# A hybrid decoder layer on one core: the attention half of the out-projection summed ahead of the delta rule, with weight buffers reused by halves

## What is computed

```python
def hybrid_mixer(...):
    proj = x @ w_in                                   # q_a k_a v_a | q_d k_d v_d | b a z
    o_attn = sliding_window_sink_attention(q_a, k_a, v_a, attn_sinks)      # 512 columns
    o_dn = gated_delta_rule(q_d, k_d, v_d, g, beta)                        # 512 columns
    o_dn = rms_norm(o_dn) * dn_norm_g * silu(z_d)
    return jnp.concatenate([o_attn, o_dn], axis=-1) @ w_out                # 1024 x 1024
...
h = layer_norm(alpha * h + mix, ln1_g, ln1_b)
ffn = peer_ffn(h, peer_w_query, sub_keys, expert_u, expert_v)
h = layer_norm(alpha * h + ffn, ln2_g, ln2_b)
```

## Time and profile before

| what | us |
|---|---|
| median of 3 runs | 3261.68 |
| the profiled execution, its own time | 3272.0 |
| its span, first to last instruction | 3270.2 |
| PE busy (matmul) | 2437.8 (75%) |
| DVE busy | 2231.2 (68%) |
| POOL busy | 1183.3 (36%) |
| ACT busy | 1140.2 (35%) |
| mean granted TensorE clock | 0.872 of full speed |

### The profile page before, as it was taken

How to read it: one execution, slowest core, us unless ns; L and a number is a source line. 1 busy time by engine, 2 the same in 40 slices (tenths; PEclk the granted TensorE clock), 3 DMA queues, 4 the chain that set the end, 5 groups by cost and what they waited for, 6 DMA issues and landing times.

```text
span 3270.2 us, 37892 instructions
## 1 busy us (share of the span) xinstructions
PE 2437.8 (75%) x11896; PEld 1362.5 (42%) x11896; DVE 2231.2 (68%) x5593; ACT 1140.2 (35%) x3499; POOL 1183.3 (36%) x1028
## 2 busy tenths in 40 slices
PE   8888778867788677877778777776778667776554
PEld 7675335534356233543446433553345323341111
DVE  3367765896559865797558875588656986579444
ACT  3213532344332533335233353234423253322222
POOL 0022543244422444334432344333443244333452
PEclk9899898988999888888989898997899879887777
DMA  8069999999999999999999999999999999989997
GB/s 331 13 235 399 408 421 397 384 394 383 398 403 396 384 415 404 385 403 379 421 383 398 388 402 398 387 379 396 386 407 383 392 387 415 397 350 356 421 421 315
DMA packets 189000, 1235.90 MB, mean 378 GB/s; under 512 B 21752, under 2 KB 21880, under 8 KB 54656
## 3 DMA queue, kind: packets, MB, share of 16 engines
q0 software_dynamic: 147456, 1073.81, 80.9%
q1 hardware_dynamic: 39168, 154.32, 12.0%
q10 hardware_dynamic: 2176, 5.36, 0.4%
HBM read 1229.21 MB, written 4.19 MB: 377 GB/s over the span
## 4 chain that ended last, share of the span: by engine, by line
PE 35%; DMA 26%; DVE 20%; ACT 9%; issue 8%; POOL 2%; DVEq 0%; POOLq 0%; ACTq 0%; SPq 0%
DMA ring<-in_uv,expert_used 22%; PE expert_sum L880 15%; DVE ring L1557 9%; PE bank L587 8%; PE bank L576 5%; DMA chunk<-in_weights 4%; POOL ring L526 2%; ACT diag L1138 2%; PE bank L594 1%; PE bank L704 1%; DVE arena L1280 1%; ACT arena L997 1%; ACT h_raw L1131 1%; PE bank L599 1%; ACT L1131 1%
## 5 line engine op out<-in xcount | busy, mean ns | idle before, releaser
L526 POOL DMA_INDIRECT ring<-in_uv,expert_used x1024 | 1183.1, 1155 | 2056.1 <-PE expert_sum L880 1568.2
L880 PE MATMUL expert_sum<-ring,diag 128*64 128x512 f32 x4096 | 1208.1, 719 | 686.6 <-ACT diag L1138 686.1
L1557 DVE CUSTOM_DVE_ANT_0 ring<-ring,x_pair 128x1024 f32<-128x1024 f32 x1024 | 1230.6, 1223 | 567.7 <-DMA ring<-in_uv,expert_used 562.4
L880 PEld LDWEIGHTS expert_sum<-ring,diag 128*64 128x64 f32 x4096 | 313.2, 156 | 1329.7 <-issue 1315.8
L1131 ACT ACTIVATE h_raw<-h_raw 128x2 f32<-128x2 f32 x512 | 104.2, 204 | 1555.6 <-DVE h_raw L1557 1554.7
L1138 ACT ACTIVATE diag<-const,h_raw 128x64 f32<-128x64 f32 x1024 | 292.7, 333 | 1.8 <-PE expert_sum L880 1.8
L1134 ACT ACTIVATE h_raw<-h_raw,gate_used 128x1 f32<-128x1 f32 x1024 | 245.6, 286 | 16.7
L587 PEld LDWEIGHTS bank<-oT,chunk 128*128 128x128 f32 x1376 | 156.4, 192 | 22.7 <-issue 22.7
L587 PE MATMUL bank<-oT,chunk 128*128 128x128 f32 x1376 | 162.4, 277 | 0.0
L576 PE MATMUL bank<-chunk,oT 128*128 128x256 f32 x464 | 116.6, 401 | 31.4 <-DMA chunk<-in_weights 30.6
L1280 DVE MAX8 arena<-arena 128x8 f32<-128x128 f32 (+1 forms) x384 | 103.8, 326 | 41.4 <-ACT arena L1089 36.2
(11 more groups left out here) (255 smaller groups left out, 2663.3 us busy)
## 6 DMA issues: line engine op xcount, KB each, us to landing
chunk<-in_weights SPq DMA_DIRECT2D x228, 512.0 KB, 10.7
ring<-in_weights SPq DMA_DIRECT2D x16, 1024.0 KB, 18.8
ring<-in_uv,expert_used POOLq DMA_INDIRECT x1024, 11.5
chunk<-in_weights SPq DMA_DIRECT2D x5, 1024.0 KB, 19.6
x<-in_x SPq DMA_DIRECT2D x8, 512.0 KB, 13.7
out<-oT ACTq DMA_DIRECT2D x8, 512.0 KB, 8.4
o_cat<-in_xT SPq DMA_DIRECT2D x7, 512.0 KB, 15.2
xT_even<-in_xT SPq DMA_DIRECT2D x4, 512.0 KB, 10.0
```

The costliest lines, as they stand in the source:

```text
L526: pool.indirect_dma_start(out=ring[:, (j % RING) * 2 * D:(j % RING + 1) * 2 * D], out_offset=None, in_=io["uv"], in_offset=bass.IndirectOf ...
L880: mm = pe.matmul(expert_sum[i][c * SPAN:(c + 1) * SPAN, :], diag[:, (j % DIAGS) * SPAN:(j % DIAGS + 1) * SPAN], ring3[:, j % RING, D + i * ...
L1557: dve.tensor_tensor_reduce(u, u, x_pair[:, (j % 2) * D:(j % 2 + 1) * D], 1.0, 0.0, ALU.mult, ALU.add, h_raw[:, j:j + 1]).then_inc(dotted.s ...
```

## The change

1. PE turns attention's half of `o_cat` right after mark att_o (it waits for `att_out`, and uses bank 5); ACT copies it to `oT` after its copies of the keys and values, ahead of the work of norms.
2. Between the marks norms and decay, PE makes the sums over k-tiles 0 to 3 of all four out-chunks, into banks 4 and 5. This takes the place of `keep_busy(early, 6)` of block 0.
3. DVE adds alpha times x to them (two operations) right after L1379, ahead of mark decay; the kk matmuls into bank 5 wait for this (`half_added`).
4. After the delta rule PE turns only the second half of `o_cat` and sums over k-tiles 4 to 7 only. DVE's two operations there stay, as plain additions.
5. Weight halves become units of their own: four places of 512 KB, used in turn, each half loaded when the half four loads earlier has been used. The order for the out-projection is the first halves of its four chunks, then the second halves.
6. One pair each moves from marks norms and decay to softmax and turn_p.

```diff
 EARLIER = dict(
-    rope=1, gates=1, taps1=1, scores=2, taps2=1, softmax=1, turn_p=1, att_o=2,
-    norms=2, decay=2, kk=1, ...
+    rope=1, gates=1, taps1=1, scores=2, taps2=1, softmax=2, turn_p=2, att_o=2,
+    norms=1, decay=1, kk=1, ...
...
+        def half_place(g):
+
+            return chunk[g % 4 // 2][:, g % 2 * KT * W // 2:(g % 2 + 1) * KT * W // 2]
...
             def load(g):
-                c = LOADS[g][0]
-                before = LOADS[g - 2] if g > 1 else (...)
-                for half in range(2):
-                    cols = slice(half * KT * W // 2, (half + 1) * KT * W // 2)
-                    if half == 0:
-                        sp.wait_ge(half_used, USED[before])
-                    else:
-                        sp.wait_ge(*used(*before))
-                    alone(sp)
-                    sp.dma_start(chunk[g % 2][:, cols], io["weights"][c][:, cols]).then_inc(chunk_in[g % 2][half], 16)
+                c, _, half = LOADS[g]
+                if g > 3:
+                    last = LOADS[g - 4]
+                    sp.wait_ge(half_used, HALF_USED[last[0], last[1], last[2]])
...
+                alone(sp)
+                sp.dma_start(half_place(g), io["weights"][c][:, half * KT * W // 2:(half + 1) * KT * W // 2]).then_inc(half_in[g % 4], 16)
...
-                for c in range(IN_CHUNKS, CHUNKS):
+                for half in range(2):
+                    for c in range(IN_CHUNKS, IN_CHUNKS + OUT_CHUNKS):
+                        load(LOAD_OF[c, n + 1, half])
+                for c in range(IN_CHUNKS + OUT_CHUNKS, CHUNKS):
                     if c not in KEPT:
-                        load(LOAD_OF[c, n + 1])
+                        for half in range(2):
+                            load(LOAD_OF[c, n + 1, half])
...
+            def half_tokens_out(m, c, out, act, half):
+
+                half_there(c, m, half)
+                w, ks = half_of(c, m, half), HALVES[half]
+                for k in ks:
+                    mm = pe.matmul(out, act[:, k, :], w[:, k % 4, :], start=(k == ks[0]), stop=(k == ks[-1]))
+                half_done(mm)
...
                 mark("att_o")
-
+                pe.wait_ge(*att_out.at(n, 1))
+                turn_each(bank[5], o_cat[:, 0:512]).then_inc(o_T.sem, 1)
...
                 mark("norms")
+                pe.wait_ge(*o_Tc.at(n, 1))
+                for c in range(OUT_CHUNKS):
+                    half_tokens_out(n, IN_CHUNKS + c, bank[4 + c // 2][:, (c % 2) * W:(c % 2 + 1) * W], oTv, 0)
                 mark("decay")
 
-                keep_busy(early, 6)
                 pe.wait_ge(*qk_normed.at(n, 1))
...
                 turn_each(bank[3], kn).then_inc(ktok.sem, 1)
+                pe.wait_ge(*half_added.at(n, 1))
                 each_head(bank[5], kn, kn).then_inc(ktok.sem, 1)
-                pe.wait_ge(*att_out.at(n, 1))
...
-                for i in range(2):
-                    turn_each(bank[3 + i], o_cat[:, i * 512:(i + 1) * 512]).then_inc(o_T.sem, 1)
+                turn_each(bank[4], o_cat[:, 512:1024]).then_inc(o_T.sem, 1)
                 mark("o_T")
                 pe.wait_ge(*o_Tc.at(n, 2))
                 for c in range(OUT_CHUNKS):
-                    tokens_out(n, IN_CHUNKS + c, bank[3 + c // 2][:, (c % 2) * W:(c % 2 + 1) * W], oTv)
+                    half_tokens_out(n, IN_CHUNKS + c, bank[3 + c // 2][:, (c % 2) * W:(c % 2 + 1) * W], oTv, 1)
...
@@ scalar: att_o @@
                 act.copy(vrows[:, 0, :], vrows[:, 1, :]).then_inc(att_kept.sem, 1)
+                act.wait_ge(*stored.at(n, -16))
+                act.wait_ge(*o_T.at(n, 1))
+                act.copy(oT[:, 0:512], bank[5][:, :]).then_inc(o_Tc.sem, 1)
...
@@ scalar: o_T @@
-                act.wait_ge(*stored.at(n, -16))
-                for i in range(2):
-                    act.wait_ge(*o_T.at(n, i + 1))
-                    act.copy(oT[:, i * 512:(i + 1) * 512], bank[3 + i][:, :]).then_inc(o_Tc.sem, 1)
+                act.wait_ge(*o_T.at(n, 2))
+                act.copy(oT[:, 512:1024], bank[4][:, :]).then_inc(o_Tc.sem, 1)
...
@@ vector: behind L1379 @@
+                dve.wait_ge(*x_loaded.at(n, 16))
+                for i in range(2):
+                    dve.wait_ge(half_used, HALF_USED[IN_CHUNKS + 2 * i + 1, n, 0])
+                    ins = stt(out=x1[:, i * 512:(i + 1) * 512], in0=x1[:, i * 512:(i + 1) * 512], scalar=ALPHA,
+                              in1=bank[4 + i][:, :], op0=ALU.mult, op1=ALU.add)
+                ins.then_inc(half_added.sem, 1)
                 mark("decay")
...
@@ vector: out @@
-                dve.wait_ge(*x_loaded.at(n, 16))
+                dve.wait_ge(*half_added.at(n, 1))
                 for i in range(2):
                     dve.wait_ge(*used(IN_CHUNKS + 2 * i + 1, n))
-                    ins = stt(out=x1[:, i * 512:(i + 1) * 512], in0=x1[:, i * 512:(i + 1) * 512], scalar=ALPHA,
-                              in1=bank[3 + i][:, :], op0=ALU.mult, op1=ALU.add)
+                    ins = tt(x1[:, i * 512:(i + 1) * 512], x1[:, i * 512:(i + 1) * 512], bank[3 + i][:, :], ALU.add)
```

More of the change, by code:

```diff
@@ L72, in in_pass, with _use @@
     return kinds
-USED, LOAD_OF, LOADS, COPIED, LAST_COPY = {}, {}, [], {}, []
-def _use(c, blocks, streamed):
-    for m in blocks:
[L83 to L87, removed]
+HALF_USED, LOAD_OF, LOADS, COPIED, LAST_COPY = {}, {}, [], {}, []
+def _use(c, blocks, streamed, halves=(0, 1)):
+    for half in halves:
+        if streamed:
+            LOADS.append((c, blocks[-1], half))
+    for m in blocks:
+        for half in halves:
+            HALF_USED[c, m, half] = len(HALF_USED) + 1
+            if streamed:
+                LOAD_OF[c, m, half] = len(LOADS) - len(halves) + halves.index(half)
 for _c in range(IN_CHUNKS):
@@ L95 @@
     LAST_COPY.append(len(COPIED))
-    for _c in range(IN_CHUNKS, CHUNKS):
+    for _half in range(2):
+        for _c in range(IN_CHUNKS, IN_CHUNKS + OUT_CHUNKS):
+            _use(_c, [_n], _n > 0, (_half,))
+    for _c in range(IN_CHUNKS + OUT_CHUNKS, CHUNKS):
         _use(_c, [_n], _n > 0 and _c not in KEPT)
@@ L287, in build @@
         x_loaded = signal("x_loaded", 16)
-        chunk_in = [[sem(f"chunk_in{i}_{half}") for half in range(2)] for i in range(2)]
+        half_in = [sem(f"half_in{i}") for i in range(4)]
         half_used = sem("half_used")
-        chunk_used = sem("chunk_used")
         in_copied = sem("in_copied")
@@ L350, in build @@
         residual = signal("residual", 1)
+        half_added = signal("half_added", 1)
         ln1_rows = signal("ln1_rows", 2)
@@ L493, in _ @@
                     for c in KINDS[kind]:
-                        load(LOAD_OF[c, blocks[0]])
+                        for half in range(2):
+                            load(LOAD_OF[c, blocks[0], half])
                 sp.wait_ge(*rows_staged.at(n + 1, 0))
@@ L566, in half_there, with half_done @@
                 else:
[L567 to L568 removed]
+                    g = LOAD_OF[c, m, half]
+                    pe.wait_ge(half_in[g % 4], 16 * (g // 4 + 1))
+            def half_done(mm):
+                mm.then_inc(half_used, 1)
             def tokens_out(m, c, out, act):
[L572 removed]
                 for half, ks in enumerate(HALVES):
                     half_there(c, m, half)
+                    w = half_of(c, m, half)
                     for k in ks:
[L576 to L577 removed]
+                        mm = pe.matmul(out, act[:, k, :], w[:, k % 4, :], start=(k == 0), stop=(k == KT - 1))
+                    half_done(mm)
[4 more added lines that the diff above has]
+                    mm = pe.matmul(out, act[:, k, :], w[:, k % 4, :], start=(k == ks[0]), stop=(k == ks[-1]))
+                half_done(mm)
             def channels_out(m, c, outs, act):
[L581 removed]
                 for i, out in enumerate(outs):
@@ L585, in channels_out @@
                             half_there(c, m, half)
+                        w = half_of(c, m, half)
                         for k in ks:
-                            mm = pe.matmul(out, w[:, k, i * P:(i + 1) * P], act[:, k, :], start=(k == 0), stop=(k == KT - 1))
+                            mm = pe.matmul(out, w[:, k % 4, i * P:(i + 1) * P], act[:, k, :], start=(k == 0), stop=(k == KT - 1))
                         if i == 1:
-                            mm.then_inc((half_used, chunk_used)[half], 1)
+                            half_done(mm)
             def each_head(out, lhsT, rhs):
```

17 lines of the change are left out of this document (9 added, 8 removed).

## The result

The changed kernel's median is 3240.22 us (3239.71 to 3245.28, 5 runs) against 3267.75 us (3259.92 to 3273.38, 5 runs) of the kernel before in the same group: ratio 0.9929, 95% interval 0.9911 to 0.9947. Two later groups of runs, on two different chips, gave 0.9933 (0.9909 to 0.9957) and 0.9902 (0.9876 to 0.9928). The profiled execution took 3245.28 us with a span of 3243.5, 26.7 less than before.

The account below looks back on a forecast made before the run. DMA engines bound the steady part, the compute chain bounds block 0. Gains of 17.5 + 5 + 4.5 = 27.0 us from the profiled 3272.0, or from the median 3261.7, give 3235 us; range 3208 to 3272.

Parts of the forecast that it names:

- signs named for being right: Out stretch windows 54 instead of 62 us at 405 GB/s or more; delta rule windows about 5 us longer, at 420.
- End of the mixer: Delta rule's end to x1_T: chain 8.2 us shorter, two chunk loads gone; 2.5 us a block net, 17.5 in seven.
- The delta rule: Its full DMA engines take over 5.0 us of weight loads a block, so its windows grow by that.
- Attention's output to kk: Steady blocks: pairs spread more evenly return ring places sooner; gain of 5 us taken, out of 0 to 17.1.
- Half loads as cover for kk's delay: Kk starts about 5 us later; ring places and four half loads cover it, costing nothing; 35 us without cover.
- Query stage: Stretch from x1_T to the end of the query sums; the forecast's sum has no term for it.
- Block 0: Compute chain counts in full: 3.1 us lost before L1386, 7.6 saved at the out-projection, net 4.5; gathers start that much earlier.
- Nothing in the steady part: Rival, chance 0.28: the lower DMA rate moves along with the loads; only block 0's 4.5 us remain, 3257 us.
- All of it: Rival, chance 0.12: all of the DMA shortfall goes, 29.3 + 17.1 + 4.5 = 51 us, 3211 us.
- Slower: Rival, chance 0.10: half sums at half clock between norms and decay starve the gathers' ring, 30 us lost, 3292 us.

Follow-up runs that it names:

- experiment 9: Changed kernel with one pair moved from mark dn to mark kv1, ahead of DVE's chain behind the delta rule: 3239.72 us, ratio 0.9931.
- experiment 10: Changed kernel with one pair moved from dn to kv1 and PE's L631 products issued behind mark dn instead of ahead: 3224.88 us, ratio 0.9886.
- experiment 11: Changed kernel with one pair moved from dn to kv1 and out-chunk 3's second half loaded only at the delta rule's end: 3234.50 us, ratio 0.9904.
- experiment 4: Changed kernel with all second halves of out-chunks loaded only at the delta rule's end, repeated beside the changed kernel on one chip: 3248.83 us, ratio 0.9959.
- experiment 1: Changed kernel with the old table of pairs (softmax and turn_p 1, norms and decay 2): 3256.62 us, ratio 0.9985.
- experiment 2: Kernel before with only the new table of pairs (softmax and turn_p 2, norms and decay 1): 3263.47 us, ratio 1.0014.
- experiment 3: Changed kernel with all second halves of out-chunks loaded only at the delta rule's end, first time: 3244.98 us, ratio 0.9956.
- experiment 6: The changed kernel unaltered, run again as a yardstick: 3238.23 us, ratio 0.9933 to the kernel before.
- experiment 12: The changed kernel unaltered, third time, as the yardstick of its group: 3235.33 us, ratio 0.9902 to the kernel before.
- experiment 8: Changed kernel with 20 instead of 9 idle PE products behind block 0's out-projection: 3245.38 us, ratio 0.9954.
- experiment 7: Changed kernel with second halves of out-chunks 2 and 3 loaded only at the delta rule's end, 0 and 1 as before: 3236.90 us, ratio 0.9925.

## Why the prediction came out as it did

The time was right (27 us of gain forecast, 27.5 measured in the same group), the parts were not. Their errors cancel, and that is luck. The range of 3208 to 3272 us was wide, too: it takes in the kernel before at 3267.75. Two of the signs named for being right failed: the out stretch stayed at 385 to 402 GB/s where 405 or more was asked for, and the delta rule's windows didn't grow.

- **End of the mixer, taken 17.5: 4.0 came** (up to 11.4 by the other traces of the changed kernel). The chain did get shorter (windows of 54.7 to 57.3 us, predicted 54; 6.2 us less a block, predicted 8.2) and PE's waits for weights went. The step that failed is the one from "the chain is shorter than the DMA work" to "the DMA engines are full": the wait that remained is DVE's chain at L1476 to L1484, which holds the dot products of pairs that have landed, and PE's L631 after it. Experiments 9 to 11 bear this out: one pair and eight products in another order take it from 18.9 to 8.5, and with the pair moved it is the blocks with slow L631 that fall short. And I took the loads that left the stretch for a pure gain, where they had filled part of the hole (experiment 4: 2.2 us short with them).
- **The delta rule, 5.0 us longer: it was 3.1 shorter** (627.7 us in seven blocks, 649.5 before), still at 420. The loads did come into it: its DMA work (length minus shortfall) is 89.5 us a block, against 85.7 with the pairs alone moved and 85.3 with the loads late. The step that failed is another. Before, it was 92.6 a block: with the pairs alone moved, 7 us of gathers had left this window, and I had taken the pairs to change nothing here ("Their total up to kk is the same"). Why it is 7 us isn't shown. The length of a window between landmarks of compute says little where the DMA engines set the pace.
- **Attention's output to kk, taken 5 of 17.1: 20.7 came.** The mechanism was named (ring places are returned sooner, the half loads lie over the delay of kk), the size was wrong. By experiments 1 to 4 the pairs and the loads are both needed, so that the hole and the loads meet. I gave half the clock as a reason to expect little; it has a share in the size of the hole (experiment 1), and the change has 0.93 in all seven blocks here. But with the loads in place blocks at 0.87 lose little as well, at most 1.3 us in experiments 6 and 12.
- **Half loads as cover for kk's delay, costed at nothing: right**, and just enough. Without them 36 us more fall short up to the end of the delta rule, against the 35 that I wrote; the time grew by only 13.5 us by medians, as the late loads fill another gap (experiment 4).
- **Query stage, costed at nothing: 6.9 came**, the rest gave back 5.6. No experiment bears on these, and one execution of each kernel can't show them.
- **Block 0, 3.1 lost in front and 7.6 saved behind: 3.6 and 7.3.** Its net of 4.5 did not show in the profiled pair: the first gather came 8.8 us sooner (185.0, 193.8 before; 3.9 of it from attention's sums at a better clock), and at 240 us only 3.2 us of work were left of it, at 400 us 1.5. In experiments 1 and 3, with the same block 0 and the first gather at 184.4 and 183.4, over 9 us more work than before was delivered at 240 us and 8 at 400. So the gain in front was there. The profiled execution has the stop on ACT that is told below; but so has experiment 9, with the first gather at 184.9, and there 5.4 and 7.2 us were left. The stop is then at most a part of the loss, and the rest stays open. Experiment 8 leans to the view that the chain counts.
- **Rivals.** "Nothing in the steady part" missed: 26 us came there. "All of it" missed because the end of the mixer kept 18.9 to 26.3 us. The rule from the Trainium skill, "Perfetto Trace Analysis", section "DMA Optimizations", that splitting may let a task complete sooner if the DMA engines are generally idle, I had read the other way round: no gain if they are busy. The page doesn't say that, and the loads are of 512 KB in both kernels, so it is their place and not their size that changed. These engines had a share of 0.98 in block 5 before kk and still moved only 367 GB/s; the trace of the change disagrees with the outcome that I had read out of the page. "Slower" missed because the half sums ran at the full clock in every block. The Trainium skill, "TensorE: Matmul & The Clock Gate", section "HAM oscillation — how this bites in real kernels", says that bursts between waits run throttled: the trace disagrees for the half sums (7.17 us in each of blocks 1 to 7) and agrees for L631 in three blocks of experiment 9 (7.19 us).

## What to carry to other kernels

Where a DMA ring is nearly full, add up by stage what it falls short of its full rate, and lay transfers with freedom in their order (prefetches of weights) over the time in which the ring gets no places back; moving work and moving loads paid only together here. Shortening a chain of compute brings little if the instruction that returns the ring place still stands behind it in some queue, so look at each engine's order just there, and put the returning work ahead of whatever has slack.

## What the runs showed that was not expected

- **A stop of 3 to 4 us on ACT beside the first gathers.** Block 0's copies of query sums came 9.0 us apart, but the fourth came 12.7 after the third in the changed kernel; in experiments 6 to 9 it was 11.9 or 12.0, in the kernel before and all other runs 9.0, among them the changed kernel itself in experiment 12. So it is not the change. It goes by chip or by group of runs: experiments 6 to 9 are the four traces of one chip, and none of the eight traces of the two other groups of experiments has it. Timeline, changed kernel and experiment 1:

```profile
195.24 0.58 ACT L1111 COPY arena<-bank 128x512 f32<-128x512 f32 x1 [10.23 <-remote]
```

```profile
190.84 0.58 ACT L1111 COPY arena<-bank 128x512 f32<-128x512 f32 x1 [6.43 <-PE bank L610]
```

  The ninth gather followed the first by 31.2 us there, by 25.2 before. The profile names no wait of the program for it; what it waits for is open.
- **The same eight products take 3.69 to 4.23 us in four blocks and 7.19 in three** of one execution (experiment 9), with the same 3.0 us of idle time ahead of the sum in front of them (blocks 1 and 4 above). So the level of the clock behind a wait couldn't be told from the wait here, and it is part of the price.
- **The runs spread more than the first ones showed.** Of the kernel before, 3242.5 to 3280.8 us in the 29 runs of one group; of the changed one 3229.8 to 3249.1 in 10. Differences of 5 us between two kernels of one group were out of reach even with ten or twelve runs each.
